# Second network of a two-network kernel: the output projection taken by row groups, and the second tile's compressed attention started without waiting for the convolution

## The chip, the cores and the metric

The kernel runs on one core of one Trainium2 chip. The metric is the device time of one execution in microseconds (us). The engines are named as in the profile: PE (matrix multiply), DVE (vector), ACT (scalar, activations), POOL and SP (which issues the DMAs). Every engine works through its own list of instructions in order and waits at semaphores for the others.

## What is computed

One sequence of 256 tokens with 1024 features goes through a first network of two layers and then through a second one of two layers. Only the middle part of a layer of the second network matters here:

```python
proj = x @ w_in[l]
(h_a, b_a, c_a, uv, q, kc, vc, ksl, vsl, kw, vw, gl) = jnp.split(proj, split_points, axis=-1)
y_a = short_conv(h_a, b_a, c_a, conv_w[l])
y_b = gmlp_spatial(uv, ...)
y_c = nsa_attention(q, kc, vc, ksl, vsl, kw, vw, gl, ...)
mix = jnp.concatenate([y_a, y_b, y_c], axis=-1) @ w_out[l]
x = layer_norm(ALPHA * x + mix, ln2_g[l], ln2_b[l])
```

`y_a` has 256 columns (rows 0 and 1 of `w_out`, counted in blocks of 128), `y_b` 256 (rows 2 and 3), `y_c` 512 (rows 4 to 7). The attention has three branches: a compressed one with 15 keys a head, and two with the full 256 keys. The queries are cut into two tiles of 128.

## The kernel before, in words

**Weights.** A weight arrives as a unit of 128 x 2048 numbers (SP issues its DMA). ACT rounds it to the high part (`high`, line 1798) and DVE subtracts to get the low part in two halves (`low`, line 2022). Each product is three matmuls: high by high, high by low, low by high (lines 217 to 219, or 224 to 226 where they add onto a bank that is already filled). Three raw units and three split ones are held.

**A plan made in advance.** The function `script` writes one list of steps, and each engine runs its own share of every step in that order. Where two streams of work are laced together, `mix` (line 248) does it by costs: each `yield` names the cost of the steps just written, and the second stream gets steps until its account reaches 1.04 times (`SHARE2`) that of the first. So the list order, and with it the order in each engine's queue, comes from these costs and not from measured time.

**The stage around the change** is laced at line 1356. Its first stream is linear work; the second is `nsa()` (line 1249), the attention. From the last quarter of unit 204 (the convolution's third input) on, the linear stream is:

- **A0**: the last quarter of unit 204.
- **A1 to A4**: the four quarters of unit 205, `lin_conv2` (line 1192). Between them `beside` (line 1218) puts the convolution's DVE steps: its gate ahead of A2, its two sets of taps ahead of A3 and A4, `conv_end` ahead of A5, `conv_split` ahead of A6 (this one has an ACT and a DVE half).
- **A5 to A12**: eight quarters of the output projection, `lin_out` (line 1351), each 2 x 3 matmuls of 128x512 onto a bank. Four of them use unit 206, four use unit 207.

With a unit's second quarter the unit two further on is begun (`spread`, line 349): ACT's `high` of 207 follows A2, of 208 follows A6, of 209 follows A10. The two halves of that unit's `low` follow the third and the fourth quarter.

A bank of the output projection is first filled with the layer's input by ACT: `seed` (line 1837), two banks per column half. `take_acc` (line 1346) issues them: the first pair ahead of A4, the second pair ahead of A7.

In the attention, a task of the full branches makes these steps in turn: scores (line 1617) with DVE's maximum (line 2131) and ACT's exponentials (line 1868); `scale` on DVE (lines 2159 to 2168); `weigh`, which is transposes on PE (line 1509) and copies on ACT (line 1876); values on PE (line 1651). Tasks are laced by `slots` (line 742), so that scale and scores of the next task come together. From A0 on I call the main pieces

- **M1** weigh, **M2** scale and scores, **M3** values, **M4** weigh, **M5** scale and scores, **M6** values (the last of tile 0), **M7** weigh, **M8** scale, **M9** values, **M10** weigh, **M11** nothing (an empty slot), **M12** values.

The weighs M1 and M4 are half as long as M7 and M10. The compressed attention of one tile, `compressed` (line 1268), has six side pieces:

- **S1** `cmp_scores` (PE line 1757, then DVE line 2360), **S2** `cmp_max` (DVE, line 2366), **S3** `cmp_exp` (ACT, line 1952), **S4** `cmp_mask` (DVE, from line 2373), **S5** `cmp_turn` (a transpose on PE, line 1764, then DVE, line 2386), **S6** `cmp_values` (PE, line 1773).

After each main piece one side piece may follow (line 1314). Tile 0's six are done before A0. Tile 1's wait for the mark that `conv_split` sets. The list before is therefore, for each linear piece and what follows it:

```
A0 M1 M2 | A1 M3 M4 | A2 M5 | A3 M6 M7 | A4 M8 M9 | A5 M10 | A6 S1 M11
A7 S2 M12 | A8 S3 S4 | A9 S5 S6 | A10 | A11 | A12
```

In A5 to A12 the eight quarters are, before: unit 206 rows 2 and 3 (`y_b`) of tile 0 and tile 1 in column half 0, rows 0 and 1 (`y_a`) of tile 0 and 1 in column half 0; then unit 207, the same for column half 1. Column half 1, with the second pair of seeded banks, is first written by A9.

The costs that the account goes by are the numbers at the `yield`s: 1.44 (`PART`) for each A and for M8 and M11, 0.44 for M1 and M4, 0.88 for M7 and M10, 1.6 for M2 and M5, 0.45 for M3 and M6, 0.9 for M9 and M12; 0.5, 0.5, 0.5, 0.9, 0.3 and 1.0 for S1 to S6. When A0 has been written the linear account stands at 23.04 and the attention's at 22.64.

Of the kernel before, what the change touches and what calls it, by code (L numbers as in the profile page):

```python
# [24 lines left out]
UNIT = 2048  # L25
SHARE1 = 0.4
SHARE2 = 1.04
PART = 1.44
# [200 lines left out]
def dense(banks):  # L229
    for b in banks:  # L230
        b.dense = True
    return banks
# [59 lines left out]
def chain(*gens):  # L292
    for g in gens:
        if callable(g):
            g = g() or ()
        yield from g


class Plan:
# [21 lines left out]
    def add(self, kind, *args):  # L321
        self.steps.append((kind, args))
# [128 lines left out]
def script(P):  # L451

    m, I = P.m, P.I
    XT, O1, O2, X = P.XT, P.O1, P.O2, m["x"]
    PB, TH, TM, RT, ER, ET = P.PB, P.TH, P.TM, P.RT, P.ER, P.ET
    C = P.C
    add = P.add
# [169 lines left out]
            seed(b, *((i, n) if c is None else (n, c)))  # L627
        return pair

    def out_part(w, acc, src_events, c, r=0, ks=(0, 2), beside=None):  # L630
        segs = [(lambda a, n=n: a[:, 0:UNIT].rearrange("p (k c) -> p k c", k=4)[:, 2 * n:2 * n + 2, :],
                 w[(r + k0) * 128:(r + k0 + 2) * 128, c * 512:(c + 1) * 512].rearrange("(k p) c -> p k c", p=128)) for n, k0 in enumerate(ks)]
        g = P.unit(segs, UNIT, True)
        for n, k0 in enumerate(ks):
            for i in range(2):
                end = n == i == 1
                if n and not i and beside:
                    beside()
                add("n_part", g, acc[i][c], O1, r + k0, 2 * n, i, src_events[n], False, False, [("used", g)] if end else None, True)
                P.spread(g, 2 * n + i)  # L640
                if not end:
                    yield PART
        yield PART
# [82 lines left out]
    def score_pair(q, k, js, i, bias, mask, rs, q_events):  # L726

        bs, ers = [PB.take() for _ in range(2)], [ER.take() for _ in range(2)]
        K = 128 * (i + 1)
        if i:  # L730
            dense(bs)
        add("score_pair", bs, [[q[64 * hh:64 * hh + 64, j, i * 128:(i + 1) * 128] for hh in range(2)] for j in js],
            [[k(hh, j)[:, 0:K] for hh in range(2)] for j in js], mask, i, q_events)
        for hh in range(2):
            if bias is not None:
                add("biased", bs[hh], 2, K, bias(hh, js, K), ers[hh], P.small(2), rs[hh])
            else:
                add("soft", bs[hh], 2, K, P.small(2), ers[hh], rs[hh])
        PB.give(*bs)
        return ers  # L740
# [316 lines left out]
    def swiglu(l, which, before, setup=iter(())):  # L1057
        def gate_up(j):
            return [(lambda a, g=g: a.rearrange("p (k g c) -> p k g c", k=8, g=2)[:, :, g, :],
                     I[f"ffn{which}_{n}_2"][l][:, j * 128:(j + 1) * 128].rearrange("(k p) f -> p k f", p=128))  # L1060
                    for g, n in enumerate(("gate", "up"))]
        f = ("second", l, which)
        n = 1 if which == 1 else 3
        return ffn(f, gate_up, I[f"ffn{which}_down_2"][l], 0.5, before, (I[f"ln{n}_g_2"][l], I[f"ln{n}_b_2"][l]), setup)
# [25 lines left out]
    def second(l, o, nxt):  # L1090
# [3 lines left out]
        acc, tail = swiglu(l, 1, ("ht read", ("first", 1) if l == 0 else ("second", 0, 2), 10))  # L1094
# [123 lines left out]
        def beside(a, b):  # L1218
            b = b()
            for x in a:  # L1220
                yield x
                next(b, None)
            for _ in b:
                pass
# [24 lines left out]
        def nsa():  # L1249
            obs, sums, split = {}, [0, 0], []  # L1250

            def part(i, kind, *args):

                if not sums[i]:
                    obs[i], = dense([PB.take()])
                ob = obs[i]
                add(kind, ob, *args[:2], sums[i] == 0, sums[i] == 4, *args[2:])
                sums[i] += 1
                if sums[i] == 5:
                    split.append(i)  # L1260

            def full():
                for i in split:
                    add("o_split", obs[i], range(4), (), (), [O1[:, z, 4:8, i * 128:(i + 1) * 128] for z in (0, 1)], [o1_before], [("o1 nsa", l, i)], 1.0 / ALPHA)
                    PB.give(obs[i])
                split.clear()

            def compressed(i):
                er, mx, rs = ER.take(), P.small(8), P.small(8)
                bs = [PB.take() for _ in range(2)]  # L1270
                add("cmp_scores", l, i, bs, er, kcs)
                PB.give(*bs)
                yield 0.5
                add("cmp_max", l, i, er, mx)
                yield 0.5
                add("cmp_exp", l, i, er)
                yield 0.5
                add("cmp_mask", l, i, er, rs, gts)
                yield 0.9
                tb, et = PB.take(), ET.take()  # L1280
                add("cmp_turn", l, i, er, tb, et)
                PB.give(tb)
                ER.give(er)
                yield 0.3
                part(i, "cmp_values", l, et)
                ET.give(et)
                yield 1.0

            def task(i, bno, jp):

                js, T = (2 * jp, 2 * jp + 1), i + 1
                rs, rc = P.small(4), P.small(4)

                def K(hh, j):
                    return KS[64 * hh:64 * hh + 64, bno - 1, :]
                if jp:
                    yield from at.until("q")
                ers = score_pair(Q, K, js, i, None, causalb, [[rs[:, 2 * hh + n:2 * hh + n + 1] for n in range(2)] for hh in range(2)],
                                 [("q nsa", l, jp), ("k nsa", l), "masks"])
                yield 1.1 + 0.5 * i  # L1300
                gate = gts[:, 24 * i:24 * i + 24].rearrange("p (g j b) -> p g j b", g=2, j=4)[:, :, 2 * jp:2 * jp + 2, bno]
                add("scale", ers, rs, rc, (("gates", l), gate), 128 * T)
                yield 0
                ets = turned(ers, i)
                yield 0.44 * T
                yield from at.until("v")
                outs = [(hh, lambda ob, hh=hh: ob.ap[64 * hh:64 * hh + 64, jp * 256:(jp + 1) * 256].rearrange("p (n q) -> p n q", n=2),
                         VS[:, mt, (bno - 1) * 128 + hh * 64:(bno - 1) * 128 + (hh + 1) * 64],
                         ets[hh].ap[:, 0:2 * T * 128].rearrange("p (n t q) -> p n t q", n=2, t=T)[:, :, mt, :]) for mt in range(T) for hh in range(2)]
                part(i, "values_t", ets, outs, [("v nsa", l)], [("win read", l)])  # L1310
                ET.give(*ets)
                yield 0.45 * T
            main = slots([task(i, bno, jp) for jp in range(2) for i in range(2) for bno in (1, 2)], (-1, 0, -2, -1))
            side = chain(lambda: early, at.until("q"), lambda: compressed(0), at.until("conv"), lambda: compressed(1))
            for cost in main:
                if cost is IDLE:
                    yield IDLE
                    continue
                yield cost
                ready = list(split)  # L1320
                x = next(side, IDLE)
                if x is not IDLE:
                    yield x
                if ready:
                    full()
            for x in side:
                full()
                yield x
            full()

        at = Line()

        def both():
            yield from at.until("cmp")
            yield from compress(comp["b"])
# [4 lines left out]
        early = weave([gmlp(0), gmlp(1), both()], 3)  # L1340
# [3 lines left out]
        acc = [[], []]  # L1344

        def take_acc(c):
            for i, b in enumerate(acc_pair(c=c)):
                acc[i].append(b)
            PB.spare = None if c else False

        def lin_out():
            for c in range(2):
                if c == 0:
                    P.flush()
                yield from out_part(I["w_out_2"][l], acc, [[("o1 gmlp", l)], [("o1 conv", l)]], c, ks=(2, 0), beside=None if c else lambda: take_acc(1))
        mix(chain(lin_v(), lin_q(1), lin_conv(), beside(chain(lin_conv2(), lin_out()), conv)), steps, SHARE2)
        P.both = False
        P.o1_read = ("o1 read", "second", l)
        layer_norm(acc, out_end(I["w_out_2"][l], acc, [[("o1 nsa", l, i)] for i in range(2)], P.o1_read, heads=True))
        acc, tail = swiglu(l, 2, ("ht read", ("second", l, 1), 10), nxt)  # L1360
# [1114 lines left out]
```

## Time and profile before

| | us |
|---|---|
| median of 3 runs | 1993.8 (1993.3 to 1993.98) |
| the profiled execution's own time | 1992.34 |
| span of its trace, first to last instruction | 1990.5 |
| PE busy | 1973.2 |
| DVE busy | 1246.2 |
| ACT busy | 911.0 |
| POOL busy | 99.7 |

The span is what the trace shows; 1.8 us of the execution lie around it. The granted clock of PE was 1.000 on average. An engine's busy time is the sum of the stretches in which an instruction of it ran; a PE that is busy 99% of the span can still lose time in a few places, and these are found in the list of waits and in the order of starts.

### The profile page before, as it was taken

How to read it: one execution, taken by the hardware profiler on the slowest of the kernel's cores; microseconds unless marked ns; L12 is line 12 of the kernel's file. 1: busy time of each engine (PE TensorE's matmuls, PEld its weight loads, DVE VectorE, ACT ScalarE, POOL GpSimd, SP SyncE). 2: the span in 40 equal slices, each digit the busy share in tenths (PEclk: the TensorE clock that was granted, in tenths of full speed). 3: DMA queues.
4: the chain of work that ended last, by engine and by line, in shares of the span. 5: the costliest groups of instructions: out<-in, count | busy, mean ns of one | idle time of the engine just before them, and what ended most of it. 6: DMA issues, size and time to landing. Idle time of an engine off the chain costs nothing.

```text
span 1990.5 us, 31852 instructions
## 1 busy us (share of the span) xinstructions
PE 1973.2 (99%) x13856; PEld 1800.0 (90%) x13856; DVE 1246.2 (63%) x1769; ACT 911.0 (46%) x1218; POOL 99.7 (5%) x84
## 2 busy tenths in 40 slices
PE   8999999999999999999999999999999999999998
PEld 6888999999888999999999989799999998979997
DVE  6566656565656766655565567665566556776555
ACT  4445444444445544444444445544444444554442
POOL 0000001000100000100100020010010002001000
PEclk9999999999999999999999999999999999999999
DMA  7544566666544455696566646468657665646663
GB/s 288 172 145 144 173 208 193 198 209 191 173 166 149 141 177 197 196 264 183 179 204 189 190 151 171 111 195 257 190 170 212 189 187 148 178 109 195 186 189 106
DMA packets 421414, 361.85 MB, mean 182 GB/s; under 512 B 29393, under 2 KB 361497, under 8 KB 421273
## 3 DMA queue, kind: packets, MB, share of 16 engines
q1 hardware_dynamic: 421272, 359.80, 58.9%
q8 instruction: 109, 1.79, 0.4%
q14 instruction: 33, 0.26, 0.0%
HBM read 358.72 MB, written 1.05 MB: 181 GB/s over the span
## 4 chain that ended last, share of the span: by engine, by line
PE 94%; DVE 4%; ACT 1%; DMA 0%; issue 0%; SPq 0%; DVEq 0%
PE ps L217 22%; PE ps L219 22%; PE ps L218 22%; PE ps L224 8%; PE ps L226 8%; PE ps L225 8%; PE ps L1509 2%; DVE hl L2022 1%; PE ps L1617 1%; PE ps L1651 1%; ACT hl L1798 0%; DMA raw<-in_w_in 0%; DVE small L2127 0%; PE ps L1622 0%; PE ps L1689 0%; DVE er L2125 0%
## 5 line engine op out<-in xcount | busy, mean ns | idle before, releaser
L2022 DVE TENSOR_TENSOR hl<-raw,hl 128x1024 fp32r<-128x1024 f32 (+1 forms) x532 | 722.3, 1390 | 385.6 <-ACT hl L1798 384.4
L217 PE MATMUL ps<-xt,hl 128*128 128x256 f32 (+1 forms) x2672 | 754.3, 282 | 0.0
L218 PE MATMUL ps<-xt,hl 128*128 128x256 f32 (+1 forms) x2672 | 746.1, 279 | 0.0
L219 PE MATMUL ps<-xt,hl 128*128 128x256 f32 (+1 forms) x2672 | 745.9, 279 | 0.0
L1798 ACT ACTIVATE hl<-raw 128x2048 fp32r<-128x2048 f32 (+1 forms) x337 | 613.8, 1829 | 219.1 <-PE ps L226 158.6
L217 PEld LDWEIGHTS ps<-xt,hl 128*128 128x128 f32 (+1 forms) x2672 | 501.0, 187 | 5.4 <-issue 2.3
L218 PEld LDWEIGHTS ps<-xt,hl 128*128 128x128 f32 (+1 forms) x2672 | 501.0, 188 | 3.2
L219 PEld LDWEIGHTS ps<-xt,hl 128*128 128x128 f32 (+1 forms) x2672 | 500.8, 187 | 0.2
L224 PE MATMUL ps<-hl,o 128*128 128x512 f32 x656 | 261.5, 399 | 0.0
L226 PE MATMUL ps<-hl,o 128*128 128x512 f32 x656 | 259.0, 395 | 0.0
L225 PE MATMUL ps<-hl,o 128*128 128x512 f32 x656 | 258.8, 395 | 0.0
L217 PE MATMUL ps<-hl,xt 128*128 128x512 f32 (+1 forms) x576 | 207.0, 359 | 1.5 <-DVE hl L2022 1.4
L219 PE MATMUL ps<-hl,xt 128*128 128x512 f32 (+1 forms) x576 | 202.1, 351 | 0.0
L218 PE MATMUL ps<-hl,xt 128*128 128x512 f32 (+1 forms) x576 | 202.0, 351 | 0.0
L1846 ACT ACTIVATE th<-ps 128x256 f32<-128x256 f32 x132 | 50.7, 384 | 329.4 <-PE ps L219 329.4
L226 PEld LDWEIGHTS ps<-hl,o 128*128 128x128 f32 x656 | 123.5, 188 | 28.9
L224 PEld LDWEIGHTS ps<-hl,o 128*128 128x128 f32 x656 | 123.4, 188 | 27.2 <-issue 1.5
L225 PEld LDWEIGHTS ps<-hl,o 128*128 128x128 f32 x656 | 123.9, 189 | 25.5
L217 PEld LDWEIGHTS ps<-hl,xt 128*128 128x128 f32 x576 | 108.4, 188 | 19.9 <-DVE hl L2022 3.0
L219 PEld LDWEIGHTS ps<-hl,xt 128*128 128x128 f32 x576 | 108.3, 188 | 16.0
L218 PEld LDWEIGHTS ps<-hl,xt 128*128 128x128 f32 x576 | 108.5, 188 | 14.4
L2105 DVE SCALAR_TENSOR_TENSOR tm<-th,ps 128x256 f32<-128x256 f32 x132 | 55.5, 420 | 99.6 <-ACT th L1846 95.4
(197 smaller groups left out, 1576.5 us busy)
## 6 DMA issues: line engine op xcount, KB each, us to landing
raw<-in_w_in SPq DMA_DIRECT2D x83, 1024.0 KB, 5.0
raw<-in_w_ffn_in SPq DMA_DIRECT2D x88, 512.0 KB, 5.1
raw<-in_ffn_gate SPq DMA_DIRECT2D x88, 512.0 KB, 3.9
raw<-in_ffn_up SPq DMA_DIRECT2D x88, 512.0 KB, 5.2
raw<-in_ffn_down SPq DMA_DIRECT2D x44, 1024.0 KB, 5.1
raw<-in_w_ffn_out SPq DMA_DIRECT2D x22, 1024.0 KB, 5.0
raw<-in_w_out SPq DMA_DIRECT2D x24, 512.0 KB, 4.8
raw<-in_w_branch_a SPq DMA_DIRECT2D x8, 1024.0 KB, 5.0
```

Of the source, the lines that this page charges most:

```text
L217: e.matmul(out, l[0], r[0], start=start, stop=False)
L218: e.matmul(out, l[0], r[1], start=False, stop=False)
L219: return e.matmul(out, l[1], r[0], start=False, stop=stop)
L224: e.matmul(out, l[0], r[0], start=False, stop=True, skip_group_check=True)
L225: e.matmul(out, l[0], r[1], start=False, stop=True, skip_group_check=True)
L226: return e.matmul(out, l[1], r[0], start=False, stop=True, skip_group_check=True)
L1509: ins = e.transpose(b.ap[:, k * 128:(k + 1) * 128], x, ident)
L1617: ins = e.matmul(b.ap[:, n * K:(n + 1) * K], qs[n][hh], ks[n][hh], start=n == 0, stop=mask is None and n == 1)
L1798: e.activation(m["hl"][:, k % NHL, 0, c], m["raw"][:, k % NRAW, c], ACT.Copy).then_inc(s.high.up(*([("high", k, h)] if parts == 2 else [(" ...
L1846: e.activation(tha, ga, ACT.Tanh, scale=0.5).then_inc(done.up(th.full), 1)
L2022: e.tensor_tensor(lo[:, c], m["raw"][:, k % NRAW, 0:n][:, c], hi[:, c].bitcast(F), ALU.subtract).then_inc(s.low.up(("low", k), *([("low", ...
L2105: e.scalar_tensor_tensor(tma, tha, 1.0, ga, ALU.add, ALU.mult).then_inc(done.up(th.free), 1)
```

## The change

The projection's quarters are regrouped, and the wait for the convolution is dropped from the side stream. A unit of `w_out` now holds one pair of row blocks for both column halves, in place of two pairs for one half. The quarters A5 to A8 (unit 206) are rows 2 and 3 for column half 0, tile 0 and 1, then column half 1, tile 0 and 1; A9 to A12 (unit 207) are rows 0 and 1 in the same order. The call that seeds the second pair of banks still stands ahead of A7.

```diff
+    def out_rows(w, acc, src_event, r, beside=None):
+        segs = [(lambda a, c=c: a[:, 0:UNIT].rearrange("p (k c) -> p k c", k=4)[:, 2 * c:2 * c + 2, :],
+                 w[r * 128:(r + 2) * 128, c * 512:(c + 1) * 512].rearrange("(k p) c -> p k c", p=128)) for c in range(2)]
+        g = P.unit(segs, UNIT, True)
+        for c in range(2):
+            if c and beside:
+                beside()
+            for i in range(2):
+                end = c == i == 1
+                add("n_part", g, acc[i][c], O1, r, 2 * c, i, [src_event], False, False, [("used", g)] if end else None, True)
+                P.spread(g, 2 * c + i)
                 if not end:
                     yield PART
         yield PART
...
-            side = chain(lambda: early, at.until("q"), lambda: compressed(0), at.until("conv"), lambda: compressed(1))
+            side = chain(lambda: early, at.until("q"), lambda: compressed(0), lambda: compressed(1))
...
         def lin_out():
-            for c in range(2):
-                if c == 0:
-                    P.flush()
-                yield from out_part(I["w_out_2"][l], acc, [[("o1 gmlp", l)], [("o1 conv", l)]], c, ks=(2, 0), beside=None if c else lambda: take_acc(1))
+            P.flush()
+            yield from out_rows(I["w_out_2"][l], acc, ("o1 gmlp", l), 2, lambda: take_acc(1))
+            yield from out_rows(I["w_out_2"][l], acc, ("o1 conv", l), 0)
```

`out_part` stays for the first network and only loses its `beside` argument.

## Rows read from the trace of the kernel before

**Rows 1.** The page: the span, and the chain that ended last by engine.

```profile
span 1990.5 us, 31852 instructions
PE 94%; DVE 4%; ACT 1%; DMA 0%; issue 0%; SPq 0%; DVEq 0%
```

**Rows 2.** Timeline of PE, layer 0: start, us, engine, line, [idle before <- releaser].

```profile
1263.70 0.65 PE L1651 MATMUL ps<-et,v 128*64 128x256 f32 x4
...
1264.69 0.37 PE L217 MATMUL ps<-xt,hl 128*128 128x256 f32 x1
...
1266.28 1.13 PE L1617 MATMUL ps<-k,q 64*128 64x256 f32 x8
...
1267.49 0.37 PE L217 MATMUL ps<-xt,hl 128*128 128x256 f32 x1
...
1275.49 1.25 PE L1509 MATMUL ps<-cst,er 128*128 128x128 f32 x8 [0.72 <-DVE er L2168]
1276.50 0.48 PE L224 MATMUL ps<-hl,o 128*128 128x512 f32 x1
...
1278.07 1.07 PE L1757 MATMUL ps<-small,q 64*128 64x15 f32 x16
...
1284.58 0.27 PE L1764 MATMUL ps<-cst,er 128*120 128x128 f32 x1
1285.63 1.13 PE L1773 MATMUL ps<-et,gb 120*128 120x256 f32 x4 [0.78 <-DVE et L2386]
1286.41 0.59 PE L224 MATMUL ps<-hl,o 128*128 128x512 f32 x1
```

**Rows 3.** Timeline of PE, layer 1: the first of its two waits.

```profile
1769.77 1.26 PE L1509 MATMUL ps<-cst,er 128*128 128x128 f32 x8 [0.72 <-DVE er L2168]
```

**Rows 4.** Timeline of DVE, layer 0, from the end of M1 on.

```profile
1260.54 0.76 DVE L2168 TENSOR_TENSOR er<-er,small 128x256 f32<-128x256 f32 x2
1262.29 1.29 DVE L2131 TENSOR_REDUCE small<-ps 128x2 f32<-128x512 f32 x2 [0.99 <-PE ps L1622]
1263.50 0.68 DVE L2298 TENSOR_TENSOR zb<-th,ps 128x512 f32<-128x512 f32 x1
...
1268.87 0.34 DVE L2307 TENSOR_SCALAR tm<-zb,small 128x256 f32<-128x256 f32 x1
...
1270.17 1.22 DVE L2022 TENSOR_TENSOR hl<-raw,hl 128x1024 fp32r<-128x1024 f32 x1
...
1274.34 0.17 DVE L2159 RECIPROCAL small<-small 128x4 f32<-128x4 f32 x1
...
1275.96 0.68 DVE L2315 TENSOR_TENSOR tm<-tm,ps 128x512 f32<-128x512 f32 x1
...
1279.19 0.35 DVE L2360 TENSOR_TENSOR er<-ps,cst 128x60 f32<-128x60 f32 x2 [0.56 <-PE ps L1757]
...
1282.52 0.27 DVE L2373 TENSOR_REDUCE small<-er 128x8 f32<-128x120 f32 x1
...
1283.47 0.28 DVE L2381 TENSOR_TENSOR er<-er,small 128x120 f32<-128x120 f32 x1
```

**Rows 5.** Timeline of ACT, layer 0: exponentials, copies, high part, seeds.

```profile
1263.02 0.47 ACT L1868 ACTIVATE er<-ps,small 128x256 f32<-128x256 f32 x1 [1.56 <-DVE small L2131]
...
1264.83 0.68 ACT L1876 ACTIVATE et<-ps 128x256 f32<-128x256 f32 x2
...
1276.18 1.20 ACT L1876 ACTIVATE et<-ps 128x512 f32<-128x512 f32 x2 [3.39 <-PE ps L1509]
...
1277.80 1.90 ACT L1798 ACTIVATE hl<-raw 128x2048 fp32r<-128x2048 f32 x1
1279.60 1.11 ACT L1837 ACTIVATE ps<-xs 128x512 f32<-128x512 f32 x2
```

**Rows 6.** Two stretches after the last matmul: us, PE, PEld, DVE, ACT, POOL busy, PEclk, DMA.

```profile
1984.00:1989.00 5.00, 0.00 (x0) 0.00 (x0) 3.75 (x7) 0.00 (x0) 0.54 (x1) 1.00 0.19 69
1989.00:1990.00 1.00, 0.00 (x0) 0.00 (x0) 0.00 (x0) 0.00 (x0) 0.00 (x0) 0.56 0.61 232
```

More of the change, by code:

```diff
@@ L628, in acc_pair, with out_part @@
         return pair
-    def out_part(w, acc, src_events, c, r=0, ks=(0, 2), beside=None):
+    def out_part(w, acc, src_events, c, r=0, ks=(0, 2)):
         segs = [(lambda a, n=n: a[:, 0:UNIT].rearrange("p (k c) -> p k c", k=4)[:, 2 * n:2 * n + 2, :],
@@ L636, in out_part @@
                 end = n == i == 1
-                if n and not i and beside:
-                    beside()
                 add("n_part", g, acc[i][c], O1, r + k0, 2 * n, i, src_events[n], False, False, [("used", g)] if end else None, True)
                 P.spread(g, 2 * n + i)
+                if not end:
+                    yield PART
+        yield PART
+    def out_rows(w, acc, src_event, r, beside=None):
[9 more added lines that the diff above has]
+                P.spread(g, 2 * c + i)
                 if not end:
```

## The prediction, made before the changed kernel ran

> **What bounds the kernel now.** I read the page's head and its chain first: PE makes up 94% of the chain that ended last, in a span of 1990.5 us [rows 1]. So a change pays only where PE stands still, or where PE gets less to do. Then I read PE's timeline in the stage of the change. There PE waits twice. M10's transposes start 0.72 late, waiting for a DVE multiplication of scale (M8), and S6 starts 0.78 late, waiting for S5's DVE part [rows 2]. Layer 1 repeats this to a hundredth [rows 3], so everything below counts twice. DVE's and ACT's timelines [rows 4, 5] then give a price for each step that moves.
>
> **Parts with one answer.** The eight quarters stay eight, with the same matmuls, and two units with as many bytes, in the same place of SP's queue; POOL has nothing here. These cost nothing. What counts is the new order.
>
> **The new order**, from the costs. A linear piece raises the attention's target by 1.44 x 1.04 = 1.50, from 23.96 after A0. The attention's account (22.64) is filled, main and side pieces in turn, until it passes the target. With S1 allowed at once: A0 takes M1, S1, M2 (25.18); A1 S2 (25.68); A2 M3, S3, M4 (27.07); A3 S4, M5 (29.57); A4 S5, M6 (30.32); A5 S6, M7 (32.20); A6 M8 (33.64); A7 M9 (34.54); A8 M10, M11 (36.86); A9 M12 (37.76). So M5 slips from behind A2 to behind A3, M7 from A3 to A5, and S1 to S6 come in earlier.
>
> **What goes away.** S5 is followed by M6 and A5 before S6, so the 0.78 is covered. Ahead of M10 PE now has M9 and A8, and scale has fewer things before it, so the 0.72 goes too, and 0.1 to 0.2 by which M10 was slowed in its second half (1.01 from start to start [rows 2]). That is 1.6 per layer. A1 and A2 as well as A6 and A7 now adjoin, while A8 and A9 no longer do: one change between kinds of matmul fewer, which I put at 0.2 (A-quarters of twelve 256-column matmuls take 1.59 with a change [rows 2]).
>
> **First new wait: A5 for its seeds.** The seeds ahead of A4 stand in ACT's queue behind M5's exponentials, which wait for M5's maximum on DVE. Before, M5's exponentials were through early. Now DVE has S1's addition, S4 and the taps ahead of that maximum. I lay out both sides from the end of S1's matmuls.
>
> DVE and ACT, after S1's addition 0.35: scale of M2, two small operations of 0.17 and one pair of 0.76 [rows 4], 1.10; from the start of its maximum to the first exponential, 1262.29 to 1263.02, 0.73 [rows 4, 5]; four exponentials, 1263.02 to 1264.83, 1.81 [rows 5]; high of 207, which is now next on ACT, 1277.80 to 1279.60, 1.80 [rows 5]. Meanwhile DVE does the maximum (1.21 from start to start), S2, the gate (0.68) and the first taps (1.30) [rows 4], and is done before high is. Then low, 1.22; S4, 1282.52 to the end of 1283.47's operation, 1.23; scale of M5, 1274.34 to 1275.96, 1.62 [rows 4]; again 0.73 and 1.81; the first seed, half of 1.11, 0.56 [rows 5]. Sum: 0.35 + 1.10 + 0.73 + 1.81 + 1.80 + 1.22 + 1.23 + 1.62 + 0.73 + 1.81 + 0.56 = 12.96.
>
> PE on the same stretch: M2 1.21 (1266.28 to 1267.49), A1 and A2 1.59 each at most, M3 and M4 0.99 (1263.70 to 1264.69), A3 1.59, M5 1.21, A4 1.59, S5 0.27, M6 0.65 [rows 2]: 10.69. PE comes to A5 about 2.3 before its seed. A1 and A2 adjoin and matmuls overlap, so PE is rather faster than this; signals between engines add to the other side. I take 2.5. The bounds are 0 (this wait is not in the trace before, and DVE might keep up) and 3.
>
> **Second new wait: A7 for its seeds.** The pair that column half 1 needs is issued ahead of A7 as before, but A7 now writes there, where A9 did. In ACT's queue come M7's copies, conv_split, high of 208, then the seeds. From the start of the transposes to the copies 0.69 (1275.49 to 1276.18), from the copies to the seeds 3.42 (to 1279.60, the very same four things before), first seed 0.56 [rows 2, 5]: 4.67. PE has only M7 (at most 1.01) and A6 (1.57, 1276.50 to 1278.07) [rows 2], since M8 gives it nothing: 2.58. The wait is 2.1; with M7 unslowed 2.2, which I take. This hangs on no backlog: ACT cannot begin before M7's transposes. Bounds 1.8 and 2.5.
>
> **Next in line.** What stands behind the waiting matmuls on PE is the attention itself, so DVE and ACT catch up during the waits: S5's DVE part is ready before A5 ends, M8's scale (1.62) before A8 ends. The high of 209 now precedes tile 1's last split on ACT, 1.80 later than before; the output projection reads it only behind A11, A12 and tile 0's part, so I put it at nothing; without that cover it would cost up to 1.8 a layer.
>
> **Sum.** Per layer 2.5 + 2.2 - 1.6 - 0.2 = 2.9; two layers 5.8. The profiled execution (1992.34, of which 1990.5 span) would become 1998.1. The median stands 1.46 above that execution, so I forecast 1993.8 + 5.8, about 1999.6.
>
> **The clock.** PE's granted clock stayed at 1.00 through five microseconds without a matmul at the end, 1984 to 1989, and was 0.56 only in the one after [rows 6]. Waits of 2.5 are half of that, so I charge nothing for the clock; by these rows 1999.6 stands. The Trainium skill, TensorE: Matmul & The Clock Gate, section HAM oscillation, says that a wait between groups of matmuls can bring the engine back to half rate each time. By that rule the sum would have a term more, the last rival's. No row here shows it in the midst of work.
>
> **Rivals.**
> - *Only the second wait comes.* DVE and ACT gain more than 2 us on my sheet, by shorter operations or a faster start. Against it: every term is a measured row, and the order of the queues is fixed by the list. Per layer 2.2 - 1.8, together +0.8: 1994.6. It passes into "slower by over 0.2%" once the first wait is over 1.6.
> - *Neither wait comes*, the seeds are filled in time, and PE runs through: twice 1.8 off, 1990.2; with one more change between kinds of matmul saved, 1989.7. This is the side of faster. It decides at A5 and A7: ACT's seeds would have to end 2.5 and 2.2 earlier than worked out. For it only that the seeds were early before; against it the queue order, which is fixed.
> - *The change does not do what it says*: the side pieces run where they ran, because the account gives no earlier slot and the seeds were long in their banks. 1993.8. The account above speaks against it.
> - *The clock falls in the waits.* The matmul work from A5 to A12 is eight quarters of 1.57, S6 0.78 and some 4 of transposes and values [rows 2], 17 per layer; at 1.2 instead of 2.4 GHz at most 17 more, 2034; half of it, 2017.
>
> **How the numbers follow.** About 0.2%, 4.0 us, can be told from no change here: below 1989.8 is faster, above 1997.8 slower. My forecast, both waits, has 0.66, with 1997.8 to 2002.3 as its own range: from the two waits adding up to 3.8 a layer (2.0 net of the 1.8 that goes away) to the upper bounds, 3 and 2.5, with 0.5 a layer for late signals. Only the second wait 0.23; neither 0.04; no effect 0.03; the clock 0.04. Slower is 0.66 + 0.04 = 0.70, same 0.23 + 0.03 = 0.26, faster 0.04. The range reaches down to 1994.2, to take in the rival with one wait, and up to 2002.3.
>
> **What would show it.** Right: in both layers PE's list of waits loses M10 for scale and S6 for S5 and shows two waits of a 128x512 matmul on a bank for ACT's seed, about 2.5 and 2.2; S1's matmuls stand between M1 and M2; DVE's maximum of M5 starts about 3 us after its scores; seeds directly follow exponentials, then a high. Wrong: PE runs from M6 into A5 without a gap (first wait), or from A6 into A7 (second), or waits for another engine than ACT there, or a PE clock under 1.00 appears in the stage.

## The result, and the profile after

The changed kernel takes 2002.21 us in the median of six runs (2000.81 to 2003.45), the kernel before 1993.28 (1992.42 to 1993.98). The ratio is 1.0046, 95% interval 1.0037 to 1.0056: slower, by 8.9 us. On the 1993.8 that the forecast starts from, the ratio gives 2003.0, above the 1999.6 forecast and just above the range's end of 2002.3 (the median itself lies 0.1 under that end, but beside a before of 1993.28). Single executions that took over 400 us longer are left out of every figure here, two of them in the first experiment. The profiled execution took 2002.87, of which 2001.1 is span; PE is busy 99% of it, as before, and the chain that ended last is still 94% PE.

The list of waits by engine comes first: columns are the waiting engine, tile and line, the releaser, us in total, times, longest.

```profile
PE ps L224 <- ACT ps L1849: 10.3, 4, 2.9
PE ps L1521 <- DMA xs<-in_x: 5.2, 1, 5.2
PE ps L217 <- DVE hl L2034: 1.3, 1, 1.3
PE ps L1663 <- DVE small L2171: 1.0, 2, 0.5
```

M10's wait for scale and S6's wait for S5 [rows 2, 3] are gone. In their place stand four waits of an output-projection matmul for ACT's seeds, 10.3 us in total; the other three lines stand in the list of before too, with 5.1, 1.4 and 0.9. PE's timeline in layer 0 shows where (as in rows 2):

```profile
1262.59 1.07 PE L1769 MATMUL ps<-small,q 64*128 64x15 f32 x16
1263.50 1.11 PE L1629 MATMUL ps<-k,q 64*128 64x256 f32 x8
...
1276.73 0.48 PE L224 MATMUL ps<-hl,o 128*128 128x512 f32 x1 [2.92 <-ACT ps L1849]
1277.05 0.40 PE L225 MATMUL ps<-hl,o 128*128 128x512 f32 x1
1277.29 0.39 PE L226 MATMUL ps<-hl,o 128*128 128x512 f32 x1
1277.52 0.55 PE L224 MATMUL ps<-hl,o 128*128 128x512 f32 x1
1277.87 0.63 PE L225 MATMUL ps<-hl,o 128*128 128x512 f32 x1
1278.30 0.63 PE L226 MATMUL ps<-hl,o 128*128 128x512 f32 x1
1278.72 1.91 PE L1785 MATMUL ps<-et,gb 120*128 120x256 f32 x4
1280.42 1.33 PE L1521 MATMUL ps<-cst,er 128*128 128x128 f32 x8
1281.51 0.48 PE L224 MATMUL ps<-hl,o 128*128 128x512 f32 x1
...
1285.39 0.47 PE L224 MATMUL ps<-hl,o 128*128 128x512 f32 x1 [2.24 <-ACT ps L1849]
```

S1 now stands between M1 and M2, A5 waits 2.92, and A7 waits 2.24. Layer 1 has the same two to a hundredth, at 1775.50 and 1784.12. But look at the starts behind the first wait. The first four matmuls start 0.23 to 0.32 apart, those from 1277.87 on 0.43 apart, and S6 at 1278.72 takes 1.91 where it took 1.13 [rows 2]. The engine runs at half its pace for a while. The clock by stretches says so too (the columns of rows 6; PEclk stands third from the end):

```profile
1273.00:1276.00 3.00, 0.81 (x7) 0.20 (x4) 2.93 (x7) 1.83 (x9) 0.00 (x0) 1.00 0.00 0
1276.00:1277.50 1.50, 0.77 (x3) 0.68 (x4) 1.50 (x3) 1.50 (x5) 0.00 (x0) 1.00 0.00 0
1277.50:1281.00 3.50, 3.50 (x11) 2.72 (x10) 1.46 (x3) 0.12 (x1) 0.00 (x0) 0.51 0.73 213
1281.00:1290.00 9.00, 6.76 (x38) 4.79 (x37) 4.51 (x7) 4.41 (x6) 0.00 (x0) 1.00 0.25 65
```

The granted clock was 1.00 in the wait, and went to the lower level (1.2 GHz, half of 2.4) only after it, with matmuls running. It was back at full clock from 1281 on. In layer 1 the stretch 1776.0 to 1779.5 had 0.52.

DVE and ACT in layer 0, up to the seeds of A5 and A7 (as in rows 4 and 5):

```profile
1270.68 0.27 DVE L2385 TENSOR_REDUCE small<-er 128x8 f32<-128x120 f32 x1
...
1271.83 0.17 DVE L2171 RECIPROCAL small<-small 128x4 f32<-128x4 f32 x1
...
1273.44 1.28 DVE L2143 TENSOR_REDUCE small<-ps 128x2 f32<-128x512 f32 x2
...
1274.16 0.47 ACT L1880 ACTIVATE er<-ps,small 128x256 f32<-128x256 f32 x1 [3.92 <-DVE small L2143]
...
1275.98 1.13 ACT L1849 ACTIVATE ps<-xs 128x512 f32<-128x512 f32 x2
...
1281.35 1.09 ACT L1888 ACTIVATE et<-ps 128x512 f32<-128x512 f32 x2 [3.73 <-PE ps L1521]
1282.32 0.63 ACT L1948 ACTIVATE o<-tm 128x512 fp32r<-128x512 f32 x1
1282.84 1.91 ACT L1810 ACTIVATE hl<-raw 128x2048 fp32r<-128x2048 f32 x1
1284.64 1.12 ACT L1849 ACTIVATE ps<-xs 128x512 f32<-128x512 f32 x2
```

On DVE, S4 (from 1270.68) and scale of M5 (from 1271.83) stand ahead of M5's maximum, ACT idles 3.92 for that maximum, and the seeds follow the four exponentials. The second pair stands behind M7's copies, `conv_split` and `high` of unit 208.

A measure used from here on is the **stage length**, from the start of A0 to the start of A10 in PE's timeline: every kernel below has the same steps between these two, apart from the transposes that two of them add. The line of A0 before, then those of A0 and A10 after (A10 before is the last of rows 2):

```profile
1258.78 0.47 PE L217 MATMUL ps<-xt,hl 128*128 128x256 f32 x1
...
1260.46 0.47 PE L217 MATMUL ps<-xt,hl 128*128 128x256 f32 x1
...
1292.83 0.50 PE L224 MATMUL ps<-hl,o 128*128 128x512 f32 x1
```

Before it is 27.63, and 27.64 in layer 1; after it is 32.37 and 32.34: 4.74 and 4.70 more, 9.4 in both layers. The rest of the kernel is 0.5 shorter than before (0.24 between the two stages, 0.3 behind the second), which leaves the 8.9 of the medians. The two profiled executions differ by 10.5, since A0 of layer 0 also comes 1.68 later in that of after; the last section comes back to such starts.

### The profile page after: what moved, and what is told of

It reads as the page before. It is cut to its first block, busy times and chain, and to the rows that moved or that the text cites. A ratio compares the mean times of both kernels' runs of the same rounds, so it can differ in the third digit from the quotient of the medians.

```text
span 2001.1 us, 31850 instructions
## 1 busy us (share of the span) xinstructions
PE 1976.5 (99%) x13856; PEld 1803.8 (90%) x13856; DVE 1246.0 (62%) x1769; ACT 910.6 (46%) x1218; POOL 99.3 (5%) x84
## 4 chain that ended last, share of the span: by engine, by line
PE 94%; DVE 4%; ACT 2%; issue 0%; DMA 0%; DVEq 0%; SPq 0%
PE ps L217 22%; PE ps L218 21%; PE ps L219 21%; PE ps L224 8%; PE ps L226 8%; PE ps L225 8%; PE ps L1521 2%; DVE hl L2034 1%; PE ps L1629 1%; PE ps L1663 1%; ACT hl L1810 1%; DVE er L2180 0%; DVE small L2139 0%; ACT er L1880 0%; PE ps L1701 0%
## 5 line engine op out<-in xcount | busy, mean ns | idle before, releaser
L224 PE MATMUL ps<-hl,o 128*128 128x512 f32 x656 | 261.7, 399 | 10.3 <-ACT ps L1849 10.3
```

Source lines behind the costliest of these rows:

```text
L224: e.matmul(out, l[0], r[0], start=False, stop=True, skip_group_check=True)
```

## The experiments

My theory after the result: the two waits cost what I had worked out, and a term is missing, the fall of the granted clock behind a wait. Rival: the waits and the clock have nothing to do with each other, and the rest is an order on PE whose cost I had wrong.

**Row groups alone.** The changed kernel with the wait for the convolution put back.

```diff
-            side = chain(lambda: early, at.until("q"), lambda: compressed(0), lambda: compressed(1))
+            side = chain(lambda: early, at.until("q"), lambda: compressed(0), at.until("conv"), lambda: compressed(1))
```

> Row groups alone; tile 1's compressed attention still waits for the convolution. Theory (two waits for seeds, and a fall of the clock that follows the first): the first wait is gone, since M5 is back behind A2, and the clock stays at 1.00. The second wait stays but S1's matmuls now stand ahead of A7, so it is about 2.2 - 1.0 = 1.2 per layer. The two old waits (M10 for scale, S6 for S5) are back. Together +2.4 us, about 1995.7. Rival (the row groups are the costly half, whatever the side stream does): +4 us or more, and the clock falls here too.

Measured: 1996.09 us (1994.51 to 1997.11), ratio 1.0015 [1.0006, 1.0025]. A7 waits 1.18 a layer, as expected: M10, A6 and S1 now lie in front of it, so the wait is about S1's 1.0 shorter than 2.24. Both old waits are there. The rival's 4 us is excluded. But I had expected a clock of 1.00, and the profiled execution had one fall, behind that wait of layer 1 (stage lengths 28.87 and 30.42):

```profile
1776.61 0.47 PE L224 MATMUL ps<-hl,o 128*128 128x512 f32 x1 [1.18 <-ACT ps L1849]
...
1778.01 0.63 PE L226 MATMUL ps<-hl,o 128*128 128x512 f32 x1
1778.56 1.98 PE L1663 MATMUL ps<-et,v 128*64 128x256 f32 x8
```

**The earlier attention alone.** The kernel before, with the wait for the convolution dropped.

```diff
-            side = chain(lambda: early, at.until("q"), lambda: compressed(0), at.until("conv"), lambda: compressed(1))
+            side = chain(lambda: early, at.until("q"), lambda: compressed(0), lambda: compressed(1))
```

> Early compressed attention alone; the projection by columns as before. Theory: the first wait stays at 2.9 with the fall of the clock behind it (1.7 per layer), the old waits are gone (1.8), the second wait for seeds is gone because A7 writes column half 0; A7 now needs the convolution's split, at most 0.7 late. Per layer 2.9 + 1.7 - 1.8 + (0 to 0.7) = 2.8 to 3.5, together +5.6 to +7, 1999 to 2000.3. Rival (the cost lies in the row groups): within 1 us of before.

Measured: 1997.88 us (1997.27 to 2002.14), ratio 1.0026 [1.0016, 1.0037]: the median is under what I expected, though the interval reaches into it. The profiled execution (1999.12) has stages of 30.76 and 30.77, 3.1 over before and inside the expected 2.8 to 3.5, with a fall in both layers; whether the executions near 1997.6 had fewer falls can't be read from their times alone.

```profile
PE ps L224 <- ACT ps L1837: 5.8, 2, 2.9
...
PE ps L224 <- DVE small L2159: 1.3, 2, 0.7
```

The first wait belongs to this part, in full. The second, for the seeds of column half 1, is not there, since columns first write these banks at A9. A7 waits 0.69 and 0.63 instead, for DVE, within the 0 to 0.7 that I had allowed for the convolution's split. So each part brings one of the two waits, as the prediction placed them. The two excesses add up within their intervals, 1.0015 and 1.0026 against 1.0046 for both, although the waits do not: the second is 1.18 in place of 2.24 with row groups alone, and the 0.69 here has no counterpart in the changed kernel.

**The first wait filled.** The changed kernel, with 22 transposes on PE ahead of A5.

```diff
+            kb = PB.take()
+            add("keep_busy", kb, 22)
+            PB.give(kb)
             yield from out_rows(I["w_out_2"][l], acc, ("o1 gmlp", l), 2, lambda: take_acc(1))
```

> The changed kernel with 22 extra transposes of the identity (into a free bank, read by nobody) ahead of A5, some 2.3 us of matmul work inside the first wait. Theory (the clock falls because of the first wait and costs 1.7 us per layer): the waiting shrinks from 2.9 to about 0.6, the granted clock stays at 1.00, and with more work done the kernel is 3.4 us faster than the changed one, about 1998.8. Rival (the clock is no part of it; the rest of the loss beyond the two waits comes from elsewhere): the same time as the changed kernel, 2002, or slower.

Measured: 2000.41 us (1999.33 to 2002.66), ratio 1.0039 [1.0026, 1.0052]: between the two theories, so half a miss, and the interval of these five runs holds the changed kernel's 1.0046, so the time alone decides nothing. The trace (an execution of 1999.42) shows more:

```profile
1271.96 2.62 PE L1731 MATMUL ps<-cst 128*128 128x128 f32 x22
1274.95 0.47 PE L224 MATMUL ps<-hl,o 128*128 128x512 f32 x1 [0.36 <-ACT ps L1859]
...
1281.96 0.77 PE L224 MATMUL ps<-hl,o 128*128 128x512 f32 x1 [2.24 <-ACT ps L1859]
...
1283.38 0.63 PE L224 MATMUL ps<-hl,o 128*128 128x512 f32 x1
```

Behind the filled wait there is no fall in either layer, but in layer 0 the second wait, left open, is now followed by one. In layer 1 the same 2.24 is followed by none, and the stage is 30.72 long there against 32.21: a price for one fall, 1.49, from two layers of one execution.

**The second pair of seeds earlier.** The changed kernel, with this pair ahead of A5.

```diff
-            yield from out_rows(I["w_out_2"][l], acc, ("o1 gmlp", l), 2, lambda: take_acc(1))
+            take_acc(1)
+            yield from out_rows(I["w_out_2"][l], acc, ("o1 gmlp", l), 2)
```

> The changed kernel with the second pair of seeds issued ahead of A5, behind the first pair, in place of ahead of A7. Theory: the second wait (2.24 per layer) goes and nothing takes its place, since A8 and M10 cover scale; first wait and clock as in the changed kernel: 2002.2 - 4.5 = 1997.7. Rival (A7 would wait anyway, for DVE's backlog): within 1.5 us of the changed kernel.

Measured: 1995.68 us (1994.18 to 1997.68), ratio 1.0015 [1.0006, 1.0024]: better than expected. The second wait is gone and nothing has taken its place; only the 2.92 at A5 is left. One fall again, in layer 0:

```profile
1275.00:1280.00 5.00, 4.02 (x11) 3.19 (x12) 3.30 (x5) 2.99 (x7) 0.00 (x0) 0.66 0.48 139
...
1770.00:1775.00 5.00, 2.67 (x14) 2.28 (x14) 3.88 (x7) 4.23 (x13) 0.00 (x0) 1.00 0.15 41
1775.00:1780.00 5.00, 5.00 (x29) 3.59 (x28) 3.68 (x7) 3.51 (x5) 0.00 (x0) 1.00 0.64 172
```

Stage lengths 29.84 and 28.26: 1.58 for the fall. One fall in two layers, where the changed kernel's profile has two, is one reason to be below the expected 1997.7. The eleven runs lie in three groups, near 1994.3, 1995.7 and 1997.4. These steps are about the price of a fall, but the runs of before also lie in two groups 1.4 apart (last section), so which step is what was not separated.

**Both pairs earlier.** As in the last kernel, with the first pair ahead of A3 besides.

```diff
-                if n == 2:
+                if n == 1:
                     take_acc(0)
```

> The changed kernel, with the first two accumulators of the output projection seeded earlier on ScalarE: the first ahead of A3, the second ahead of A5, so that neither stands behind M5's exponentials or behind the convolution's copies. My theory: A5 and A7 then begin without a wait for their seeds, but VectorE is still behind in this stretch (S4's, M5's and S5's work stand in one queue), so that S6 comes to wait for what S5 leaves, about 2.3 us per layer; in sum 0.4 us per layer more than the kernel before, or 1994.2 us at full clock, up to 1997 if the granted clock falls after that wait. Rival, by which the place of the seeds is the only obstacle: both waits go and nothing takes their place, 1989.5 us.

Measured: 1994.0 us (1992.77 to 1995.67), ratio 1.0006 [0.9997, 1.0015], as the theory has it. The rival's 1989.5 is excluded. Neither A5 nor A7 waits, but S6 does, for S5 on DVE (and in layer 0 the clock falls there: stage lengths 29.45 and 27.97):

```profile
PE ps L1786 <- DVE et L2399: 4.7, 2, 2.4
```

So at the first wait the seeds were where the lateness was seen, not where it came from: DVE's queue is behind in this stretch, and S5's part starts 16.62 after A0 in this kernel and in the changed one (1277.04 and 1277.08). The second wait came from the place of its seeds alone, since nothing took its place in the kernel before this one.

**Both waits filled.** The changed kernel, with 22 transposes ahead of A5 as above and 15 ahead of A7.

```diff
             if c and beside:
                 beside()
+                kb = PB.take()
+                add("keep_busy", kb, 15)
+                PB.give(kb)
```

> The changed kernel with 22 transposes of a constant ahead of A5 and 15 ahead of A7, which write a bank that nobody reads at that time: they lie in the two waits, so that TensorE has matmuls to do in them and the waits themselves end when they did. My theory: the two waits cost 2.92 and 2.24 us per layer as before, and what they cost beyond that is the falls of the granted clock behind them; with the waits filled there is no fall in this stage, the granted clock is 1.00 there, the time is that of the kernel before plus 2 x (2.92 + 2.24 - 1.8 - 0.2), about 1999.8 us, and the runs lie closer together than those of the changed kernel. Rival, by which the clock has no part in it: 2002 us or more, as the changed kernel.

Measured: 1999.15 us (1997.7 to 1999.6), ratio 1.0029 [1.0018, 1.004], an excess over before of 6.0 against the changed kernel's 8.9. The two intervals still overlap a little (the changed kernel's begins at 1.0037), so the stage lengths must decide: 30.74 (the two lines first below, A0 and A10) and 30.73, both at full clock:

```profile
1258.53 0.47 PE L217 MATMUL ps<-xt,hl 128*128 128x256 f32 x1
...
1289.27 0.50 PE L224 MATMUL ps<-hl,o 128*128 128x512 f32 x1
...
1271.00:1290.00 19.00, 18.02 (x113) 13.78 (x112) 10.48 (x17) 11.32 (x21) 0.00 (x0) 1.00 0.40 111
1768.00:1787.00 19.00, 18.03 (x114) 13.77 (x114) 10.61 (x18) 11.21 (x21) 0.00 (x0) 1.00 0.41 111
```

The kernel does more work on PE than the changed one, and its stage is shorter. A5 and A7 start when their seeds are there, as before, so what is gone is the falls alone: 32.37 less 30.74, 1.6 a layer. This speaks against the rival: at full clock the new order costs what its waits and gains add up to.

**Another place for the start.** The kernel before, with tile 1's side pieces released at the second taps, between the two ends tried so far, and with S4 counted dearer in the account of costs. The two edits were not tried apart.

```diff
                 add("conv_taps", l, c, yt, cols, cols_event)
+                if c:
+                    at.mark("taps")
                 yield
...
                 add("cmp_mask", l, i, er, rs, gts)
-                yield 0.9
+                yield 1.3 if i else 0.9
...
-            side = chain(lambda: early, at.until("q"), lambda: compressed(0), at.until("conv"), lambda: compressed(1))
+            side = chain(lambda: early, at.until("q"), lambda: compressed(0), at.until("taps"), lambda: compressed(1))
```

> The kernel before (output projection by columns), with the second tile's side pieces released at the convolution's second taps, which is between the end of the convolution and the start of the attention, and with S4's VectorE cost counted as 1.3. The order is then A4 S1 M8, A5 S2 M9, A6 S3 M10, A7 S4, A8 M11, A9 S5 M12 S6. My theory: M5's maximum and exponentials stay ahead of S2 to S4, so that neither of the two new waits is there, while the waits of M10 (0.72) and of S6 (0.78) are covered by linear pieces: 1.5 to 2 us per layer less than before, 1989.4 to 1990.4 us. Rival, by which any earlier start of the side pieces makes a linear piece wait for VectorE or ScalarE: a new wait at A6 to A8 of 1 us or more per layer, 1993 to 1996 us.

Measured: 1989.84 us (1988.51 to 1990.1), ratio 0.9982 [0.9973, 0.9991]: as expected, and a little faster than both kernels. M5's maximum (1268.92) and exponentials stay ahead of S2 to S4 (from 1278.18), linear pieces cover M10 and S6, and one small wait is left:

```profile
PE ps L224 <- DVE o L2036: 0.4, 2, 0.2
```

The stage is 25.92 long, 1.7 a layer under before.

**The same with row groups, and then with early seeds.** Two kernels: the place of release just tried, put into the changed kernel; and that with `take_acc(1)` ahead of A5 as above.

> The kernel with the side pieces released at the second taps (the run before this one, 1989.84 us) and with the row groups of the change added. My theory: row groups cost only through the time at which column half 1 needs its seeds, A7 in place of A9. In that run A7 started at 1279.69 and the first of those seeds ended at 1281.67 plus half of 1.12, or 1282.2: A7 waits 2.6 us per layer, in sum 1995.0 us, and up to 1.6 more for each fall of the granted clock. Rival, by which the row groups were only in the way because the side pieces came too early: the seeds are in time and the time stays 1989.8.

> As the run before it, with the seeds of column half 1 moved ahead of A5 on ScalarE, which in the run without row groups had nothing to do from 1274.0 to 1278.2. My theory: nobody waits for seeds any more, row groups and columns then cost the same, 1989.8 us, at most 0.5 us off. Rival, by which the row groups cost something of their own (the second unit is needed in another order, or the second half is split later): 1991 us or more.

Measured: 1996.88 us (1995.53 to 1999.46), ratio 1.0021 [1.0012, 1.003], for the first; 1988.72 us (1987.74 to 1989.65), ratio 0.9981 [0.9972, 0.999], for the second. In the first, A7 waits 2.92 (2.6 expected), and the clock falls in both layers, with the time inside the expected 1995.0 plus up to 1.6 a fall. In layer 1 the first matmul behind the wait is already slow, and the clock stays low until 1784, twice as long as elsewhere (stage lengths 30.19 and 31.44):

```profile
1777.90 0.76 PE L224 MATMUL ps<-hl,o 128*128 128x512 f32 x1 [2.92 <-ACT ps L1851]
1778.47 0.63 PE L225 MATMUL ps<-hl,o 128*128 128x512 f32 x1
...
1777.00:1781.00 4.00, 3.10 (x7) 2.48 (x8) 2.54 (x7) 1.28 (x3) 0.00 (x0) 0.53 0.03 7
1781.00:1786.00 5.00, 5.00 (x21) 3.54 (x19) 0.69 (x1) 1.92 (x1) 0.00 (x0) 0.69 0.76 207
```

In the second, PE's list of waits has nothing from this stage:

```profile
PE ps L1524 <- DMA xs<-in_x: 4.9, 1, 4.9
PE ps L217 <- DVE hl L2037: 1.4, 1, 1.4
PE ps L1666 <- DVE small L2174: 1.0, 2, 0.5
```

Stage lengths 25.57 and 25.55, 2.1 a layer under before. The median is 1.1 under the expected 1989.8, but before too was 0.7 lower beside these runs than beside the kernel that the 1989.8 comes from; by ratio, row groups and columns come out alike once the seeds are in time, 0.9981 against 0.9982, each known to about 0.001. The only price of row groups seen here is that column half 1 needs its seeds at A7 in place of A9.

**Falls over all profiles.** A stage of one layer in one profiled execution is a case. In the changed kernel and the kernels above that have a wait of 1.18 us or more on an empty PE there are fourteen such cases; ten had a fall of the clock, with the wait of 1.18 the shortest before one. In the eight cases of before, both waits filled, release at the taps, and that with rows and early seeds, where no wait is over 0.78, there was none. Outside these stages and the end behind the last matmul, no stretch of 2 us reads a clock under 0.97 in any of the eleven profiles. Where one execution had a fall in one layer and none in the other, the stage lengths give its price directly: 1.55, 1.49, 1.58 and 1.48 (row groups alone, first wait filled, second pair earlier, both pairs earlier).

## Why the prediction was wrong

The sign was right (slower, 0.70). By its steps:

- **The new order** came out as the account of costs gave it. **What goes away**: both old waits went, as said. Without falls the stage grew by 30.74 - 27.63 = 3.11 while the two new waits make 5.16, so 2.05 a layer went away; forecast 1.8.
- **First new wait: A5 for its seeds.** Place and cause came out as worked out, 2.92 against 2.5. The DVE and ACT side was good: from the end of S1's matmuls (1262.59 + 1.07 = 1263.66) to the first of the two seeds (1275.98 + half of 1.13 = 1276.55) 12.9, where the sum said 12.96. The PE side was too long: from the start of M2 (1263.50) to the start of the wait (1276.73 - 2.92 = 1273.81) 10.3, where it said 10.69. M2 starts 0.16 before S1's matmuls end and A5 0.18 after that middle of the seeds, and so 12.89 - 10.31 + 0.16 + 0.18 = 2.92. I had written that PE would be faster than the sum and that signals add to the other side, and took only 0.2 for both.
- **Second new wait: A7 for its seeds.** 2.24 against 2.2.
- **Sum.** The four terms net to 3.11 a layer against 2.9. The kernel with both waits filled, which has these terms and no falls, measures 6.0 over before, against the 5.8 of the forecast. The high of 209, put at nothing, cost nothing: behind A10 the kernel got shorter. (The range's upper end, by its own terms 2 x 4.2 over 1993.8, is 2002.2 and not 2002.3.)
- **The clock. This step failed**: "so I charge nothing for the clock". The missing term is 1.6 a layer, 3.2 in all, which takes 1999.6 + 0.4 (the terms' own error) to about 2003.2, or 2002.7 with the 0.5 by which the rest got shorter; the ratio gives 2003.0. The rows chosen for it were the wrong ones. Rows 6 lie behind the last matmul, so they can't show how matmuls run after a wait, and that is where the price falls: in the changed kernel the wait itself stands at 1.00 too. They are also one execution, and not a typical one: the clock fell 5.3 us after the end of the last matmul there, but 3.5 after it in the profile of the changed kernel and 2.2 in that of row groups released at the taps, so "half of that" gave no safety to a wait of 2.5. By the Trainium skill, TensorE: Matmul & The Clock Gate, section HAM oscillation, a wait for data between groups of matmuls can put the engine back to half rate each time, in a kernel whose waits are longer than the ones here. The trace agrees that waits do this in the midst of work (10 of 14 cases), and shows besides that a wait of 2.24 or 2.92 may pass without it.
- **The rivals.** "The clock falls in the waits" was the right mechanism, with the wrong size: I let the clock stay low for all or half of the 17 us that follow. It stayed low some 3.5 (once 6.8), and about half of that is the loss. A rival with both waits and one short fall a layer was missing. "Only the second wait" and "neither wait" are excluded by the list of waits.
- **What would show it.** M5's maximum starts 3.2 after the start of its scores (1270.25), 1.7 after their end. The lost and the new waits and the place of S1 are there too. Of "seeds directly follow exponentials, then a high" only the first half is: behind the seeds ACT has another step (L1820, 1277.02), M7's copies and `conv_split` before the next high, at 1282.84. The sign named for wrong is there as well, a PE clock under 1.00 in the stage.

What stays open is why one wait is followed by a fall and the same wait in the other layer is not; that the clock falls at such different times behind the last matmul shows the same spread, but no reason for it.

## What to carry to other kernels

When PE is the bound, price a wait on it at its length, plus a chance of a fall of the clock behind it; here that was 1.5 to 1.6 us at a time (more in one case), as much as the waits that the change removed. Look for the fall in the spacing of the matmuls after a wait; the idle stretch itself may read 1.00 throughout, as here. One quiet stretch of one execution is no proof that the clock holds through a shorter one. When work is started earlier in a list that every engine follows in order, ask whose maximum or seed now stands behind it: the version with the shortest stage moved the start only halfway, so that the long chain (maximum, exponentials) kept its place, and issued the seeds while ACT had nothing to do.

## What the runs showed of the hardware that was not expected

- One fall of the granted clock to the lower level, in rows that read 0.51 to 0.52 for 3.5 us (once for 6.8), went with a single wait of 2.92, 2.36, 2.24 or 1.18. It began from 0.6 us before the matmuls resumed (row groups released at the taps, layer 1, the 0.76 at 1777.90 above) to 1.3 us after (the earlier attention alone, layer 1).
- Behind the last matmul of the kernel the clock fell 2.2 to 5.3 us after that matmul's end in the eleven profiles; the profile of before, with 5.3, is one of the two longest.
- The first matmuls of the whole kernel differ from execution to execution. In the changed kernel's profile those of line 217 to 219 from 10.16 on come 0.43 apart, in that of before, from 10.19 on, 0.23 apart, though the stretch 0 to 20 reads a clock of 1.00 in both. The runs of before fall into two groups, near 1992.2 and 1993.6. That the start makes these groups is only argued: the two fast versions' profiles fit it (spacing 0.43 and a time of 1990.02 in the upper group of one; 0.23 and 1987.74 in the lower group of the other).
